# Weights of a two-network kernel stored by the host as ready 1 MB blocks, 8 KB in a row for each partition

## The reference

```python
for l in range(2):                       # first stack: 256 context tokens and 256 tokens
    m = cond @ w_mod[l] + b_mod[l]       # 1024 x 6144
    x, xc = attention(x, xc)             # w_in, w_out
    x = layer_norm(ALPHA * x + g2 * moe(h2, w_router, b_router, w_gate[l], w_up[l], w_down[l]), ...)
for l in range(4):                       # second stack: 16 + 256 tokens
    x = x + mixer(rmsnorm(x))            # FoX attention, gated linear attention, gated delta net, FoX
    x = x + (silu(h @ gate) * (h @ up)) @ w_down_2[l]
```

## Time and profile before

| | |
|---|---|
| median of 3 runs | 3912.59 us (3911.95 to 3917.58) |
| the profiled execution's own time | 3919.4 us |
| its span, first to last instruction | 3917.6 us |
| busy share of PE, PEld, DVE, ACT | 79%, 70%, 56%, 41% |
| DMA packets, bytes | 420933, 524.39 MB |
| mean granted clock of TensorE | 0.88 of full speed |

### The profile page before, as it was taken

The page is one execution under the profiler, slowest core; times in us unless marked ns, Lnnn a source line. Parts: engine busy times, 40 slices in busy tenths (PEclk is TensorE's granted clock), DMA queues, the critical chain, the costliest instruction groups (busy, mean ns, idle before and its releaser), DMA issues. The chain is left out here.

```text
span 3917.6 us, 55129 instructions
## 1 busy us (share of the span) xinstructions
PE 3098.7 (79%) x20792; PEld 2724.8 (70%) x20792; DVE 2201.0 (56%) x3823; ACT 1618.9 (41%) x2862; POOL 88.5 (2%) x82
## 2 busy tenths in 40 slices
PE   8996766988666999676799856999366589895798
PEld 3474546887545888674699846999256579793698
DVE  0026855877564888427666365664733456636666
ACT  1133534776444777434432424334231143334433
POOL 0000001101000111000000000000000000000000
PEclk9998987999787999887899958999658889996899
DMA  9820014999203999330154301554000035450153
GB/s 348 279 75 22 1 43 166 320 320 331 97 11 108 339 344 337 95 99 1 56 173 160 128 11 65 172 161 144 29 1 1 1 119 171 127 153 0 44 182 118
DMA packets 420933, 524.39 MB, mean 134 GB/s; under 512 B 14608, under 2 KB 387424, under 8 KB 420496
## 3 DMA queue, kind: packets, MB, share of 16 engines
q1 hardware_dynamic: 408400, 499.75, 39.0%
q0 software_dynamic: 9696, 12.70, 1.0%
q10 hardware_dynamic: 2656, 9.49, 0.6%
HBM read 521.81 MB, written 21.13 MB: 139 GB/s over the span
## 5 line engine op out<-in xcount | busy, mean ns | idle before, releaser
L1670 DVE TENSOR_TENSOR W_lo<-ring,W_hi 128x1024 fp32r<-128x1024 f32 x384 | 453.0, 1222 | 44.0 <-ACT W_hi L1588 43.4
L1211 PE MATMUL ps<-H_split_hi,W_hi 128*128 128x272 f32 (+1 forms) x1408 | 411.2, 292 | 49.3 <-DVE W_lo L1315 49.3
L501 PE MATMUL ps<-ACC_part,W_hi 128*128 128x272 f32 (+2 forms) x1624 | 351.8, 300 | 77.4 <-DVE ACC_part L542 44.9
L1212 PE MATMUL ps<-H_split_lo,W_hi 128*128 128x272 f32 (+1 forms) x1408 | 409.1, 291 | 0.0
L1213 PE MATMUL ps<-H_split_hi,W_lo 128*128 128x272 f32 (+1 forms) x1408 | 406.2, 288 | 0.0
L535 DVE TENSOR_TENSOR W_lo<-ring,W_hi 128x1024 fp32r<-128x1024 f32 x198 | 232.6, 1222 | 307.0 <-ACT W_hi L511 307.0
L1588 ACT ACTIVATE W_hi<-ring 128x1024 fp32r<-128x1024 f32 x384 | 384.7, 1052 | 41.6 <-PE ps L1504 20.7
L1315 DVE TENSOR_TENSOR W_lo<-ring,W_hi 128x1024 fp32r<-128x1024 f32 x264 | 313.6, 1221 | 142.6 <-ACT W_hi L1257 142.1
L501 PEld LDWEIGHTS ps<-ACC_part,W_hi 128*128 128x128 f32 x1624 | 269.9, 193 | 85.5 <-issue 79.8
L1257 ACT ACTIVATE W_hi<-ring 128x1024 fp32r<-128x1024 f32 x264 | 259.0, 1050 | 118.8 <-PE ps L1228 75.4
L1211 PEld LDWEIGHTS ps<-H_split_hi,W_hi 128*128 128x128 f32 x1408 | 268.0, 190 | 50.9 <-issue 50.9
(11 more groups left out here) (365 smaller groups left out, 6911.6 us busy)
## 6 DMA issues: line engine op xcount, KB each, us to landing
ring<-in_w_down SPq DMA_DIRECT2D x108, 1024.0 KB, 5.5
ring<-in_w_gate_up SPq DMA_DIRECT2D x88, 1024.0 KB, 5.1
ring<-in_w_gate SPq DMA_DIRECT2D x64, 1024.0 KB, 5.5
ring<-in_w_up SPq DMA_DIRECT2D x64, 1024.0 KB, 6.0
ring<-in_w_mod SPq DMA_DIRECT2D x48, 1024.0 KB, 8.7
ring<-in_fox_w_in SPq DMA_DIRECT2D x32, 1024.0 KB, 6.0
ring<-in_gdn_w_in SPq DMA_DIRECT2D x16, 1024.0 KB, 5.6
ring<-in_gla_w_in SPq DMA_DIRECT2D x12, 1024.0 KB, 5.5
```

Of the source, the lines that this page charges most:

```text
L501: mm = pe.matmul(self.out(i), a, b, start=(k == 0 and n_part == 0), stop=(k == KC - 1 and n_part == 2))
L1211: pe.matmul(out, wh[:, k, M], Hh[:, k, X], start=(k == 0), stop=False)
L1212: pe.matmul(out, wh[:, k, M], Hl[:, k, X], start=False, stop=False)
L1670: dve.tensor_tensor(lo, c.ring[:, (self.g0 + p) % SLOTS, W], hi.bitcast(F32), ALU.subtract)\
```

## The change

The host writes each large matrix into DRAM block by block, in the order and inner layout that the ring wants: for block s and partition p, the 2048 numbers of that partition stand in a row. A load of the kernel then reads one contiguous 1 MB piece, as 128 pieces of 8 KB, in place of 1024 pieces of 1 KB (or 256 of 4 KB for the down projections). The bytes, the number of loads, their destinations in SBUF, their order, all waits and all instructions of PE, ACT, DVE and POOL stay as they are; the order of instructions on these four engines is the same row for row, and on SP the same DMAs stand in the same places with the shape 128x2048 where 128x8x256 or 128x2x1024 stood, and with three register operations fewer.

```diff
 def columns(w, c0):
-    return w[:, c0:c0 + WIDE].rearrange("(k p) m -> p k m", p=P)
+    return w[c0 // WIDE]
...
-                    src = c.dram["w_mod"][layer][:, bass.ds(i * (SLOTS * WIDE) + j * WIDE, WIDE)]
+                    src = c.dram["w_mod"][layer].rearrange("s p m -> (s p) m")[bass.ds(i * (SLOTS * P) + j * P, P), :]
...
-                    sp.dma_start(c.wide(j), src.rearrange("(k p) m -> p k m", p=P)).then_inc(c.ring_full[j], 16)
+                    sp.dma_start(c.ring[:, j, :], src).then_inc(c.ring_full[j], 16)
...
-        src = self.src[kind](offset, n % 2)
-        dst = c.ring[:, g % SLOTS, :].rearrange("p (k m) -> p k m", k=src.shape[1])
-        sp.dma_start(dst, src).then_inc(c.ring_full[g % SLOTS], 16)
+        sp.dma_start(c.ring[:, g % SLOTS, :], self.src[kind][bass.ds(slot, P), :]).then_inc(c.ring_full[g % SLOTS], 16)
...
+def ring_slots(name, a):
+
+    if name in ("w_down", "w_down_2"):
+        a = a.reshape(a.shape[:-2] + (-1, WIDE // P, P, a.shape[-1]))
+        a = np.swapaxes(a, -3, -2)
+    else:
+        n = a.shape[-1] // WIDE
+        a = a[..., 0:n * WIDE].reshape(a.shape[:-2] + (KC, P, n, WIDE))
+        a = np.moveaxis(np.moveaxis(a, -2, -4), -2, -3)
+    a = a.reshape(a.shape[:-3] + (P, SLOT)) if a.shape[-3] == P else a
+    if name in ("w_gate", "w_up", "w_down"):
+        a = a.reshape((a.shape[0], -1, P, SLOT))
+    return np.ascontiguousarray(a)
```

More of the change, by code:

```diff
@@ L1155, in load @@
         c, g = self.c, self.g0 + self.pos(kind, n)
-        offset = (lambda size: (n // 2) * size) if i is None else (lambda size: i * size + (n // 2) * size)
+        slot = n * P if i is None else i * (2 * P) + n * P
         if i is None:
@@ L2404, in experts, with slots @@
     yield Router(c, layer, t0, tn, m)
[L2407 to L2418, removed]
+    def slots(name):
+        return d[name][layer].rearrange("s p m -> (s p) m")
+    yield Experts(c, t0, tn, 2 * EXPERTS, slots("w_gate"), slots("w_up"), slots("w_down"), gates=layer + 1)
 def swiglu(c, layer, first=0):
     d = c.dram
[L2423 to L2434, removed]
+    n = D_FF // WIDE
+    gate, up = (d["w_gate_up_2"][layer][j * n:(j + 1) * n].rearrange("s p m -> (s p) m") for j in range(2))
+    yield FeedForward(c, first, T2 - first, n, gate, up, d["w_down_2"][layer].rearrange("s p m -> (s p) m"))
 def fox(c, j, first=0):
@@ L2603, in lay_out @@
         a = x[key]
-        arrays[name] = np.ascontiguousarray(a[0] if name in ONE_LAYER else a)
+        arrays[name] = ring_slots(name, a[0] if name in ONE_LAYER else a)
     def chunked(a):
```

## The result

The kernel with 8 KB pieces takes 3963.2 us (median of 4 runs, 3956.1 to 3970.2), the one before 3915.1 us beside it (4 runs, 3912.0 to 3924.4). The ratio of these runs is 1.0114, with a 95% interval of 1.0097 to 1.013 (the two medians alone would give 1.0123). I had predicted 3897 us, within 3878 to 3948, and named slower as a rival with a chance of 0.32. The profiled execution took 3956.1 us, 36.7 us more than that of before. It was the quickest of its four, and the medians lie 48.2 us apart, so what follows accounts for the difference of the two profiled executions and not for the last 11 us of the medians.

The account below looks back on a forecast made before the run. PE sets the pace, stalling repeatedly for transfers only on token rows in `Experts`. Start 0.5, `Experts` 7.8 and 7.1, stage ends 1 us: sum 16 us, so 3897 us against 3912.6, range 3878 to 3948.

Parts of the forecast that it names:

- What bounds the kernel.: PE stalls repeatedly for a transfer only in `Experts`, on token rows; at most 35.7 us to win.
- The 6.4 us after its issue: In `Experts`, PE feels only what a fetch takes beyond 6.4 us after its issue (9.2 less 2.8).
- Instructions at nothing, packets: Whole kernel: instruction changes cost zero; q1 falls to some 69,000 packets, share near 30%; a block takes 0.5 us less.
- Start: gain 0.5 us: Kernel start: the first `w_mod` block lands 0.5 us sooner (bounds 0 and 0.6), first matmul at about 12.9 us.
- `Modulation`, projections, FeedForward: 0 us: These stages are bound by PE, ACT or DVE and covered by the ring, so they gain 0 us.
- `Experts`: the step that failed: Both `Experts` stages: each fetch lands 0.6 us sooner, gaining 7.8 us in layer 0 and 7.1 us in layer 1.
- The slower rival: In `Experts`, large weight pieces hold up scatter and fetch: 16 to 47 us net loss, centre 3943 us, chance 0.32.
- Its signs: In `Experts`: fetch landing at a median over 8 us, PE's wait for rows in layer 0 at 40 us or more.
- the 9 turns of the prediction: Scatter and fetch each have 9 packets per DMA engine; each turn waits for an 8 KB weight piece, 0.26 us more.

Follow-up runs that it names:

- fetch sooner: POOL issues each fetch of token rows one expert sooner: 3867.6 us (ratio 0.9862) in the changed kernel, 3882.8 us (0.9905) in the kernel before.
- 1 KB blocks: Changed kernel's contiguous 1 MB weight blocks, but stored and loaded in 1 KB pieces: 3916.4 us, ratio 0.9991 to the kernel before.
- rows of 2 KB: Token fetch brings 2 KB pieces in place of 4 KB rows: 3903.8 us in the changed kernel, 3899.3 us in the kernel before.

## Why the prediction was wrong

*What bounds the kernel.* Right. The only stalls of PE in `Experts` were those for the token rows, and removing them (fetch sooner) gives 0.95% in the old layout and 1.4% in the new. I had the time of an expert whose rows are in time at 18.6 us; it measures 18.1, so the excess to be won was 2.7 and 1.05 us for an expert in the two layers, 26 experts with 48 us, not 35.7. The fetch sooner won some 52 us with the new layout (3919.3 to 3867.6) and 35 us with the old (3917.7 to 3882.8), where the weights then came late. The 6.4 us after its issue from which PE feels a fetch held: 11.0 us less a wait of 4.6 in the late expert above.

*Instructions at nothing, packets.* Right: 69,328 packets against about 69,000. The share of q1 came to 35.4%, not near 30%. Share times span per MB is 3.06 us before and 2.80 us after (0.390 x 3917.6 / 499.75 and 0.354 x 3954.3 / 499.75), so a block of 1.05 MB keeps the engines for about 0.27 us less, half the 0.5 us that I took. That the share fell by less than I thought is no ceiling on the rate, though: with the fetch sooner the stage holds 371 GB/s over 234.5 us. The Trainium skill, page "DMA: Bandwidth & Descriptors", section on bandwidth, puts the DRAM side at about 358 GB/s for a core. The same section ties this to both cores of a memory domain streaming, and gives 425 GB/s for a core alone with 16 MB; with this core running alone, the 371 GB/s agree with that and are past the 358.

*Start: gain 0.5 us.* Wrong, and without weight. The first matmul starts at 13.41 us; it was 13.46 before, and I had it at 12.9.

*`Modulation`, projections, FeedForward: 0 us.* Right, shown by the run that changes only these: ratio 0.9994.

*`Experts`: the step that failed.* "It shares the engines, so I take 0.6 us, between the ends." The ends were 0 and 1.1 us sooner; in layer 0 the fetch lands 1.9 us later by the median and 1.3 us later on average. I had derived both ends from engine time given free by the weights, and kept the opposite sign for a rival. But the engines' free time was not what the fetch lacked: they have more idle time after the change (share 0.81 against 0.95) and it is later. What lengthens its landing is the size of the weights' pieces beside it (1 KB blocks: no loss, 8 KB: 1.1%); that this works by turns on the engines is my explanation and not shown. My forecast for this term was -14.9 us; it measured +43.2.

*The slower rival was the right one and too small.* Its signs came: the fetch's landing over the whole run at 8.4 us (over 8 was the sign) and PE's wait in layer 0 at 43.5 us (40 and more). I centred it at 30 us. Two of its parts were off. It had the scatter late by 1.2 us and the fetch unharmed or hurt as much; in the trace the scatter is sooner by 0.6 us and the fetch carries the whole loss. And it had no term for the clock, which is a third of the loss: each wait that is followed by a stretch at 1.2 GHz costs about 1.5 us on top of itself. The kernel before had four of these already in layer 0 (spans at clock 0.92), so the term could have been read: the earlier trace rows has a clock of 0.97 for this stage.

*How the turns work is not settled.* The piece size decides (1 KB blocks: no loss), and the times at 1, 2, 4 and 8 KB grow about in proportion to it, which a turn of one piece, or of any fixed number of them, would give. The medians of the landing (8.5, 8.6, 8.6 and 10.3 us) don't show that proportion and the means (8.3, 8.5, 8.6 and 9.8 us) only roughly. The rows of 2 KB don't decide between turns and bytes. Nor is each of the 144 packets a row: q0's 4320 packets from 640 to 1000 us hold 7.53 MB, some 1840 rows of 4 KB, and the rest are skipped rows and semaphores, so the 9 turns of the prediction are not 9 equal ones. The Trainium skill, same page, section on queues, rings and completion order, says that an engine drains a whole packet of a queue, typically of some 9 to 17 descriptors, before it turns to the next. Such a packet is a group of pieces and not what the profile counts as one, and no run here shows how many pieces of a load form one. Open as well are why landings with 8 KB pieces fall into two groups (6.2 to 8.6 us, and 9.3 to 11.0) and why the change in `Experts` alone costs less than the whole.

## What to carry to other kernels

Large pieces for a bulk stream are not free for a small transfer that somebody waits for on the same DMA engines: before enlarging them, look whether a gather has slack, and read the landing of the gather and not the DMA share, which can fall while the gather gets later. Look at the single landings too: a median of 7.3 us that became 7.6 in layer 1 hid five landings of 9.3 to 10.7. First issue the small transfer early enough that its landing is hidden (here one expert sooner), and then enlarge the pieces: they cost 1.1% without the early fetch and gain 15 us with it. Price a wait of TensorE with what follows it, here 1.5 us of low clock behind many of the waits, and read the clock column of the stage before taking a small wait for a small cost.

## What the chip showed that I had not expected

- The landing of a gather of at most 128 rows of 4 KB (64 on average) beside weight pieces of 1, 2, 4 and 8 KB: medians of 8.5, 8.6, 8.6 and 10.3 us in layer 0, means of 8.3, 8.5, 8.6 and 9.8 us.
- A gather's rows of 2 KB in place of 4 KB took 2.4 us off the median beside 8 KB pieces and 0.5 us beside the old ones, and went in 80 packets in place of 144.
- Skipped rows of a gather still make packets: a fetch has 144 in layer 1 as in layer 0, with half the rows.
- The second transfer of a pair in q0 has the same landing whichever it is (10.3 us for the fetch behind the scatter, 10.3 us for the scatter behind the fetch). The first was sooner beside 8 KB pieces than beside the old ones in one pair of kernels (5.3 against 5.9 us) and later in the other (8.6 against 6.7 us, fetch one expert sooner).
- A standstill of PE of 4.6 us was followed by some 3.5 us at a granted clock of 0.50; two standstills of 2.1 us in one run ended one with and one without such a fall.
